# Expert weights as fp16 halves, split by ScalarE and GpSimd during the projection and the mixing

## The chip, the core and the metric

The program runs on one core of a Trainium2 chip as one launch. The metric is its time on the device in microseconds (us); the profile is of one execution of the same program.

## What is computed

One layer of a streaming encoder over 4096 prompt frames and 8 streams of 16 frames (33 tiles of 128 rows, 1024 wide). The change touches the layer's last part, a mixture of 32 experts of which each row takes two; rows are sorted by expert and cut into blocks of 128 rows that belong to one expert. From the reference:

```python
def mixer(h, ...):                       # in: rmsnorm(x); 2 head groups; out projection
    proj = h @ w_in
    xc, new_conv_l = causal_conv(x_lru, conv_l, lru_cw)
    hs, new_h = rglru(xc, h_l, ...)
    o, new_S = gdn_sequence(S_g, q, k, v, g, beta)
    return mixed @ w_out, ...

def expert_dispatch(xf, eidx, wts, w1, w3, w2):
    ...
    xb = xf[row_tok].reshape(n_blocks, ROW_BLOCK, D)
    def run(args):
        e, xblk = args
        return (jax.nn.silu(xblk @ w1[e]) * (xblk @ w3[e])) @ w2[e]
    yb = lax.map(run, (block_e, xb)).reshape(n_rows, D)
    contrib = yb[dest] * w_sorted[:, None].astype(yb.dtype)
    return jnp.zeros((T, D), yb.dtype).at[tok_sorted].add(contrib)
```

## The kernel before

The program has four phases, one after the other: projection, mixing, experts, combination. Each engine runs its own instruction list; semaphores order them. `SP` only issues DMA.

**Projection** (`project_phase`). 4096 rows go through in eight groups of 512, and the streams' 128 rows are a ninth group. Each group is cut into 24 chunks of 128 output columns, and each chunk is 24 fp16 matmuls on TensorE (three for each of eight slices of the inner dimension, because inputs and weights are held as a high and a low fp16 half: hi x hi, hi x lo, lo x hi). `sequence()` writes out by hand the order in which every engine goes through a group: Y and X chunks of the recurrent unit with their gates (`G`, `R`, `O`), Q chunks of the queries, keys and values with their convolution on VectorE and their SiLU (`S`), Z chunks of the output gate, `N` the squares of the next group's input and its norm, `B` the two decay columns. ScalarE copies a chunk from PSUM to `win` (L384), VectorE convolves it (L504 to L513). GpSimd does two small operations a group for the norm (L260, L263) and is otherwise idle. The tile `stage` (two slots of 512 KB) takes raw weights in the first group, where ScalarE and VectorE split `w_in` into halves.

**Mixing** (`mix_phase`). 33 tiles in a software pipeline; a table `MIX` says which step stands on which engine in which order in an iteration. The output projection is in halves as well. `X.Z64c` is a copy by ScalarE (`Zf`), `X.fh` and `X.fl` make the halves of the recurrent unit's output (`f_hi`, `f_lo`), `V.v` is a batched triangular inversion by VectorE, `R.x2` the residual sum (`x2b`), `R.r2` a norm on GpSimd (`rs`), `Q.sct0` a scatter of row numbers to `table` by GpSimd, `R.h2` a multiplication on GpSimd (`h2b`). The streams' state `S_s` (2 MB) is loaded at iteration 0 and used by the last tile.

**Experts** (`experts_phase`). 98 blocks. Table `EXPERTS`: TensorE does `up` of block b + 1 (8 fp32 matmuls over 512 columns, weights `w13`), the transposes `gT` of block b, the transposes `T0`, `T1` of the rows of block b + 2, then `d0`, `d1` of block b (4 fp32 matmuls, weights `w2`). ScalarE does `silu`, VectorE the product `mul`; `T0c` (ScalarE) and `T1c` (VectorE) copy transposed rows to SBUF, `gTc` (ScalarE) the transposed product, `d0c` and `d1c` the result. The weights of an expert (2 MB and 1 MB) lie in one of two slots; SP loads an expert's weights when `d1` of the last block that used the slot is through:

```python
sem_, value = at("d1", end, 1)
sp.wait_ge(sem_, value)
load_expert(sp, T, weights, pair * 2 + (2 + p), p)
...
arrived(pair * 2 + (2 + p), p)     # waits for both loads, then counts up `ready`
```

and `up` waits for `ready`.

**Combination** (`combine_phase`) gathers each row's two results and writes the output.

Of the kernel before, what the change touches and what calls it, by code (L numbers as in the profile page):

```python
# [50 lines left out]
M_SCALE = 4.0  # L51
OUT = 1.0 / (W_SCALE * M_SCALE)
W13, W2 = KD * 2 * FE, (FE // P) * D

# [45 lines left out]
def sequence():  # L100
# [6 lines left out]
    for m in range(3, QC):  # L107
        out += [("Q", m), ("S", m - 1)] + [("N", 0)] * (m == 6) + [("B", 0)] * (m == 9)
    return out + [("Z", 0), ("S", QC - 1), ("Z", 1), ("Z", 2), ("Z", 3)]


def project_phase(nc, T, gb, const, cols):
# [6 lines left out]
    with ExitStack() as ctx:  # L119
# [13 lines left out]
        junk = sb("junk", [P, D])  # L133
# [32 lines left out]

        ident = const[:, MATS.index("ident"), :]
# [33 lines left out]
        table_out = sem("table_out")  # L201

# [3 lines left out]
        def _(sp):  # L206
# [6 lines left out]
            sp.dma_start(const[:, :, :], T["mats"]).then_inc(setup_in, 16)  # L213
# [16 lines left out]
            with sp.Fori(2, groups) as g:  # L230
                load(g, GT)
            load(groups, 1)

# [3 lines left out]
            while done < n:  # L237
                w = min(n - done, GN)
                sp.dma_start(T["table"][done * P:(done + w) * P, 0].rearrange("(p n) -> p n", p=P),
                             junk[:, 0:w].bitcast(I32)).then_inc(table_out, 16)  # L240
# [10 lines left out]
        def _(pool):  # L251
# [13 lines left out]
            with pool.Fori(0, groups) as g:  # L265
                group(g, GT)
            group(groups, 1)
# [71 lines left out]
        def _(act):  # L339
# [19 lines left out]
            def group(g, nt, stream, following, first=False):  # L359
# [100 lines left out]
        def _(dve):  # L460
# [17 lines left out]
            def group(g, nt, stream, following, first=False):  # L478
# [6 lines left out]
                for kind, m in seq:  # L485
                    if first and block_of.get((kind, m), len(wblocks)) + 2 < len(wblocks):
                        split(block_of[kind, m] + 2)
                    if kind == "N" and following:
# [106 lines left out]
X.Z64.pe X.Z64c.act Y.outA3.pe R.r3.dve  # L595
# [3 lines left out]
MIX = [tuple(s.split(".")) for s in MIX]  # L599
ENGINES = ("pe", "act", "dve", "pool")  # L600


def mix_phase(nc, T, gb, const, cols, eid, rank, wts, base, start, tabs):
    NT, NB = tiles(), blocks()
    H = HEADS
    with ExitStack() as ctx:
# [5 lines left out]

        w_out_hi = sb("w_out_hi", [P, KD, D], FP16)
# [105 lines left out]

        w_out_raw = S_s[:, :, :, :].rearrange("p s h n -> p (s h n)").rearrange("p (k n) -> p k n", k=4)  # L720
# [3 lines left out]
        owner = {n: done[st, e] for st, n, e in MIX if st != "V"}  # L724
# [29 lines left out]
        route_columns = sem("route_columns")  # L754
        route_rows = sem("route_rows")
# [30 lines left out]

        def prologue(t):

            return t < LEAD
# [10 lines left out]
        def program(engine, begin, steps, inversion=None, after_first=None):  # L800
# [5 lines left out]
            def iteration(i):  # L806
                tiles_ = {st: tile_at(i, n) for st, n in (("E", LEAD + 1), ("F", LEAD), ("X", 1), ("Y", 0), ("R", -1), ("Q", -2))}
                for st, n, e in MIX:
                    if e != engine:
                        continue  # L810
                    if st == "V":
# [14 lines left out]
        def _(sp):  # L826
# [49 lines left out]
            def iteration(i):  # L876
# [6 lines left out]
                if x is not None:  # L883
                    sp.wait_ge(*at("x2", x[0], 1))
                    sp.dma_start(xr[:, :], T["x"][bass.ts(x[0], P), :]).then_inc(xr_in, 16)
                if valid and part == 0:
                    batch_load(b, n, min(i + LEAD, NT))
# [17 lines left out]

# [1201 lines left out]
```

## Time and profile before

| | us |
|---|---|
| median of three runs (least, most) | 3940.72 (3940.56, 3945.06) |
| profiled execution, its own time | 3933.96 |
| its span on the core | 3932.3 |
| TensorE busy | 3423.2 (87%) |
| VectorE busy | 1874.7 (48%) |
| ScalarE busy | 1318.6 (34%) |
| GpSimd busy | 816.6 (21%) |

In the profile PE is TensorE, DVE VectorE, ACT ScalarE, POOL GpSimd and SP SyncE; L12 is line 12 of the kernel. A tile is named without its buffer number, and `out<-in` says what an instruction writes and reads. The busy shares are averages over four phases with different limits. An fp32 matmul stands in the trace as two passes.

### The profile page before, as it was taken

To read this page: it belongs to the slowest core of one execution; us is meant where nothing else is said; L and a number is where in the kernel's file an instruction comes from. 1 tells how busy PE (TensorE), PEld (TensorE's weight loads), DVE (VectorE), ACT (ScalarE), POOL (GpSimd) and SP (SyncE) were. 2 spreads that over 40 slices of the span, in tenths; PEclk is the share of its full clock that TensorE was granted. 3 is DMA by queue.
4 is the path that set the end of the run, shared out by engine and by line. 5 is a ranking of instruction groups with operands and counts; after the bars stand their busy time and mean duration, and the time that the engine had idled before them with its cause. 6 is when DMAs were issued, how large, how long until landed. Compare 5 with 4: busy or idle time off the path is not lost. (4 is left out here: it accounts for less than half of the span.)

```text
span 3932.3 us, 57456 instructions
## 1 busy us (share of the span) xinstructions
PE 3423.2 (87%) x17482; PEld 2023.8 (51%) x17483; DVE 1874.7 (48%) x4755; ACT 1318.6 (34%) x2585; POOL 816.6 (21%) x1002
## 2 busy tenths in 40 slices
PE   7999999999995688889888899769999999999920
PEld 3444444444445677777777766534444444444410
DVE  6564465365454457777777776521111111111148
ACT  7465355355445133333333333211111111111112
POOL 0000000000000234544455444211111111111144
PEclk9999999999997599999999999979999999999965
DMA  4311111111012354444444444144555466553268
GB/s 142 119 38 52 60 45 48 56 48 51 35 54 81 101 149 120 129 139 142 131 122 135 134 121 128 44 183 181 190 217 219 170 235 229 192 200 120 88 253 326
DMA packets 335720, 513.88 MB, mean 131 GB/s; under 512 B 79968, under 2 KB 228928, under 8 KB 327104
## 3 DMA queue, kind: packets, MB, share of 16 engines
q1 hardware_dynamic: 252400, 279.19, 22.4%
q10 hardware_dynamic: 54288, 146.56, 9.4%
q0 software_dynamic: 28864, 86.09, 6.5%
q8 instruction: 81, 1.33, 0.1%
q14 instruction: 87, 0.71, 0.1%
HBM read 341.49 MB, written 170.26 MB: 130 GB/s over the span
## 5 line engine op out<-in xcount | busy, mean ns | idle before, releaser
L1761 PE MATMUL ebank<-w,rowsT 128*128 x1568 | 703.4, 602 | 33.7 <-SPq L1702 30.4
L300 PE MATMUL pP<-h_hi,w_hi 128*128 128x512 f16 (+1 forms) x1728 | 625.7, 366 | 31.4 <-DVE h_lo L482 16.8
L300 PE MATMUL pP<-h_hi,w_lo 128*128 128x512 f16 (+1 forms) x1728 | 625.1, 366 | 0.0
L300 PE MATMUL pP<-h_lo,w_hi 128*128 128x512 f16 (+1 forms) x1728 | 625.0, 366 | 0.0
L1761 PEld LDWEIGHTS ebank<-w,rowsT 128*128 128x128 f32 x1568 | 301.0, 193 | 421.9 <-issue 421.9
L1828 DVE TENSOR_TENSOR gu<-ebank,sil 128x256 f32<-128x256 f32 x98 | 41.6, 424 | 697.1 <-ACT sil L1796 697.1
L1779 PE MATMUL ebank<-w,guT 128*128 x784 | 353.4, 593 | 2.6 <-ACT guT L1800 2.6
L513 DVE SCALAR_TENSOR_TENSOR cv<-win,cols_sb,cv 128x512 f32<-128x512 f32 (+1 forms) x432 | 305.4, 707 | 35.1 <-issue 3.6
L1796 ACT ACTIVATE sil<-ebank 128x256 f32<-128x256 f32 x98 | 37.6, 384 | 819.3 <-PE ebank L1761 819.3
L300 PEld LDWEIGHTS pP<-h_hi,w_hi 128*128 128x128 f16 x1728 | 172.1, 100 | 221.1 <-issue 31.4
L300 PEld LDWEIGHTS pP<-h_lo,w_hi 128*128 128x128 f16 x1728 | 172.4, 100 | 188.0 <-issue 14.1
L300 PEld LDWEIGHTS pP<-h_hi,w_lo 128*128 128x128 f16 x1728 | 172.3, 100 | 183.4 <-issue 3.8
L260 POOL TENSOR_TENSOR ss<-ss,eps 128x4 f32<-128x4 f32 (+1 forms) x9 | 1.8, 197 | 1115.0 <-ACT junk L348 1115.0
L1779 PEld LDWEIGHTS ebank<-w,guT 128*128 128x128 f32 x784 | 140.9, 189 | 143.7 <-issue 143.7
L1833 DVE COPY yb<-ebank 128x512 f32<-128x512 f32 x98 | 67.8, 691 | 272.9 <-PE ebank L1779 272.9
L1729 POOL DMA_DIRECT2D idx<-table x98 | 55.0, 562 | 655.5 <-PE ebank L1751 651.0
L1732 POOL DMA_INDIRECT rows<-h,idx x98 | 95.5, 974 | 349.5 <-DMA idx<-table 344.4
L384 ACT ACTIVATE win<-pP 128x512 f32<-128x512 f32 (+1 forms) x144 | 80.1, 556 | 236.7 <-PE pP L300 234.1
L1309 POOL DMA_INDIRECT table<-tid,offs x66 | 69.7, 1056 | 330.4 <-DVE offs L1558 303.6
L1097 PE MATMUL bank<-w_out_hi,f_hi 128*128 128x512 f16 x264 | 100.4, 380 | 42.5 <-DVE lg L1497 42.5
L1751 PE MATMUL ebank<-const,rows 128*128 128x128 f32 x784 | 102.5, 274 | 27.0 <-DMA rows<-h,idx 27.0
L504 DVE COPY win<-carry 128x3 f32<-128x3 f32 x128 | 21.2, 165 | 219.8 <-ACT win L384 219.0
(328 smaller groups left out, 6219.8 us busy)
## 6 DMA issues: line engine op xcount, KB each, us to landing
w<-in_w SPq DMA_DIRECT2D x32, 2048.0 KB, 9.0
y<-yb ACTq DMA_DIRECT2D x98, 512.0 KB, 4.9
ft<-mixin SPq DMA_DIRECT2D x33, 1280.0 KB, 8.4
mixin<-qo ACTq DMA_DIRECT2D x128, 256.0 KB, 2.0
w<-in_w SPq DMA_DIRECT2D x32, 1024.0 KB, 12.3
xt<-in_x SPq DMA_DIRECT2D x33, 512.0 KB, 5.1
xr<-in_x SPq DMA_DIRECT2D x33, 512.0 KB, 5.1
x<-x2b ACTq DMA_DIRECT2D x33, 512.0 KB, 5.5
```

The lines of the kernel that those rows point to most:

```text
L300: ins = nc.tensor.matmul(pP[n % NPB][:, 0:N], w[:, k, c0:c0 + P], h[:, k, 0:N], start=(k + i == 0), stop=(k == KD - 1 and i == 2))
L384: nc.scalar.activation(window(c, 3, stream), shaped(pP[number[kind, m] % NPB][:, 0:N], stream), ACT.Copy, scale=PROJ).then_inc(*act_did.di ...
L513: ins = nc.vector.scalar_tensor_tensor(dst, window(c, j, stream), cw(j), dst, ALU.mult, ALU.add)
L1097: ins = nc.tensor.matmul(flat((YD, YE)[half]), f[:, c, :], w[:, c, half * 512:half * 512 + 512], start=(c + i == 0), stop=False)
L1309: pool.indirect_dma_start(T["table"], bass.IndirectOffsetOnAxis(ap=offs[k][:, 0:1], axis=0), tid[:, 0:1], None).then_inc(ids_out, 16)
L1729: pool.dma_start(idx[p][:, :], T["table"][bass.ds(where, P), :]).then_inc(idx_in[p], 16)
L1732: pool.indirect_dma_start(xb[p][:, :], None, T["h2"], bass.IndirectOffsetOnAxis(ap=idx[p][:, 0:1], axis=0)).then_inc(rows_in[p], 16)
L1751: ins = nc.tensor.transpose(bank[:, k * P:(k + 1) * P], xb[p][:, c * P:(c + 1) * P], ident)
L1761: ins = nc.tensor.matmul((M0, M1)[p][:, :], xT[p][:, k, :], w13[:, bass.ds(s, 1), k * 512:(k + 1) * 512].rearrange("p a n -> p (a n)"), st ...
L1779: ins = nc.tensor.matmul((OA, OB)[h][:, :], guT[p][:, k, :], w.rearrange("p a n -> p (a n)"), start=(k == 0), stop=(k == FE // P - 1))
L1828: nc.vector.tensor_tensor(gu[p][:, :], (M0, M1)[p][:, FE:2 * FE], sil[p][:, :], ALU.mult).then_inc(*did(n))
L1833: nc.vector.tensor_copy(yb[p][:, 512:], OB[:, :]).then_inc(*did(n))
```

## The change

Before the experts run, their weights are multiplied by 512 and split into a high and a low fp16 half, and the halves are written to a scratch array `ws` in DRAM. This is done in 192 pieces of 128 x 1024 fp32 (512 KB), six for each expert: 126 in the projection, 18 in each of seven groups, and 66 in mixing, two an iteration and three in every fifth one, in iterations 0 to 29. The experts then load halves (the same number of bytes) and do three fp16 matmuls in place of one fp32 matmul, so the rows and the product are split into halves too.

In the projection, ScalarE scales a piece in place (`W` in the sequence), GpSimd copies it to fp16 and subtracts, SP stores the two halves and loads the piece after the next one into the same slot. The norm of the next group stands on GpSimd after nine of the 18 pieces, and on VectorE at `M` (after Q10) instead of `N`. In mixing ScalarE makes the high half and the scaled piece, GpSimd the low half; `S_s` is their buffer, so the streams' state is loaded after the last piece. The constant matrices (704 KB) are loaded at the start of mixing, the projection loads only the identity (64 KB). `w13` and `w2` are loaded apart, each with its own `ready`, and the first waits only for `up` of the last block in its slot.

```diff
 def sequence():
     for m in range(3, QC):
-        out += [("Q", m), ("S", m - 1)] + [("N", 0)] * (m == 6) + [("B", 0)] * (m == 9)
+        out += [("Q", m), ("S", m - 1)] + [("N", 0)] * (m == 6) + [("M", 0)] * (m == 10) + [("B", 0)] * (m == 9)
...
+    for kind, m in out:
+        paced.append((kind, m))
+        if kind in "YXQZ":
+            c += 1
+            while n < NW and n < c * NW // 23:
+                paced.append(("W", n))
+                n += 1
...
# projection, SP
+            def experts(g):
+                for j in range(NW):
+                    q = (g - 1) * NW + j
+                    piece_store(q, j % 2)
+                    if not isinstance(q, int) or q + 2 < NC:
+                        piece_load(q + 2, j % 2)
...
# projection, GpSimd
+            def piece(g, j):
+                q, p = (g - 1) * NW + j, j % 2
+                turn = ((g - 1) * (NW // 2) + j // 2 + 1) * 16
+                pool.wait_ge(piece_scaled, q + 1)
+                pool.wait_ge(halves_out[p], turn)
+                pool.sem_inc(pieces_begun, 1)
+                raw = stage[:, p, :, :].rearrange("p k n -> p (k n)")
+                nc.gpsimd.tensor_copy(halves[:, p, 0, :], raw)
+                pool.drain()
+                nc.gpsimd.tensor_tensor(halves[:, p, 1, :], raw, halves[:, p, 0, :], ALU.subtract).then_inc(expert_split, 1)
+            def split(g, n):
+                for j in range(NW):
+                    piece(g, j)
+                    if j == AHEAD - 1:
+                        group(g + 1, n)
...
# projection, ScalarE
+                    elif kind == "W" and not first and not stream:
+                        raw = stage[:, m % 2, :, :]
+                        act.wait_ge(expert_in[m % 2], ((g - 1) * (NW // 2) + m // 2 + 1) * 16)
+                        nc.scalar.activation(raw, raw, ACT.Copy, scale=W_SCALE).then_inc(piece_scaled, 1)
...
 MIX = """
-X.Z64.pe X.Z64c.act Y.outA3.pe R.r3.dve
+X.Z64.pe X.Z64c.act Y.outA3.pe R.r3.dve W.hi.act W.lo.pool
...
# mixing, ScalarE and GpSimd
+            def high(q):
+                raw, hi = raws[q % 3], split[q % 3][:, 0:WC]
...
+                nc.scalar.activation(hi, raw, ACT.Copy, scale=W_SCALE)
+                act.drain()
+                nc.scalar.activation(raw, raw, ACT.Copy, scale=W_SCALE).then_inc(piece_hi, 1)
+            def low(q):
+                pool.wait_ge(piece_hi, q + 1)
+                nc.gpsimd.tensor_tensor(split[q % 3][:, WC:], raws[q % 3], split[q % 3][:, 0:WC], ALU.subtract
+                                        ).then_inc(piece_lo, 1)
...
 EXPERTS = """
-O.gT.pe O.gTc.act
-T.T0.pe T.T1.pe T.T0c.act T.T1c.dve
+O.gT.pe O.gTc.act O.gTl.dve
+T.T0.pe T.T1.pe T.T0c.act T.T0l.dve T.T1c.act T.T1l.dve
...
# experts, SP
-                    sem_, value = at("d1", end, 1)
-                    sp.wait_ge(sem_, value)
-                    load_expert(sp, T, weights, pair * 2 + (2 + p), p)
+                    for part, last_use in enumerate(("up", "d1")):
+                        sem_, value = at(last_use, end, 1)
+                        sp.wait_ge(sem_, value)
+                        load_part(sp, T, weights, pair * 2 + (2 + p), p, part)
...
# experts, TensorE: up (d0 and d1 likewise, and these wait for gTl and ready[1])
+        PARTS = ((0, 0), (0, 1), (1, 0))
-                        ins = nc.tensor.matmul((M0, M1)[p][:, :], xT[p][:, k, :],
...
+                        for i, (x, w) in enumerate(PARTS):
+                            ins = nc.tensor.matmul((M0, M1)[p][:, :], xT[p][:, x, k * P:(k + 1) * P],
+                                                   half(s, k // 2, w, k % 2 * 512),
+                                                   start=(k + i == 0), stop=(k == KD - 1 and i == 2))
```

On GpSimd in the projection's loop over groups, this stood in a group before (the two operations of the norm and the loop's end):

```order
L260 ISA
L260 TENSOR_TENSOR ss<-ss,eps 128x4
L262 REGISTER_ALU
L263 TENSOR_TENSOR rs<-ss,neghalf 128x4
L265 REGISTER_ALU
L265 COMPARE_AND_BRANCH
```

and this stands there now around the same norm, in the middle of the 18 pieces:

```order
L315 REGISTER_ALU
L316 ISA
L319 CAST halves<-stage 128x1024
L321 TENSOR_TENSOR halves<-stage,halves 128x1024
L305 REGISTER_ALU
L306 TENSOR_TENSOR ss<-ss,eps 128x4
L308 REGISTER_ALU
L309 TENSOR_TENSOR rs<-ss,neghalf 128x4
L315 REGISTER_ALU
L319 CAST halves<-stage 128x1024
L321 TENSOR_TENSOR halves<-stage,halves 128x1024
```

Nine copies and subtractions stand ahead of the norm, which was alone, and nine behind it.

On GpSimd at the end of an iteration of mixing (`ATf` is a masked attention tile, `table` the scatter, `T` an inverse tile from the batched inversion, `rs` the norm of the residual sum) before:

```order
L1276 TENSOR_TENSOR B<-Gin,const 128x512 x2
L1257 TENSOR_TENSOR ATf<-ATf,const 128x512
L1309 DMA table<-tid,offs 135296x1
L1268 TENSOR_TENSOR T<-Tin,const 128x128 x4
L1292 TENSOR_TENSOR rs<-s,eps 128x1
```

and now:

```order
L1392 TENSOR_TENSOR B<-Gin,const 128x512 x2
L1373 TENSOR_TENSOR ATf<-ATf,const 128x512
L1434 TENSOR_TENSOR split<-S_s,split 128x1024 x2
L1425 DMA table<-tid,offs 135296x1
L1384 TENSOR_TENSOR T<-Tin,const 128x128 x4
L1408 TENSOR_TENSOR rs<-s,eps 128x1
```

The low halves of two pieces stand between `ATf` and the scatter.

On VectorE in the experts, one block in the loop (its product, the copies of the transposed rows of a block further on, the copy of a result) before:

```order
L1827 REGISTER_ALU
L1828 TENSOR_TENSOR gu<-ebank,sil 128x256
L1822 REGISTER_ALU
L1823 ISA
L1824 COPY rowsT<-ebank 128x512
L1831 ISA
L1832 ISA
L1833 COPY yb<-ebank 128x512
```

and now:

```order
L1971 REGISTER_ALU
L1972 SCALAR_TENSOR_TENSOR gu<-ebank,sil 128x256
L1975 ISA
L1976 TENSOR_TENSOR guT<-ebank,guT 128x256
L1965 ISA
L1966 SCALAR_TENSOR_TENSOR rowsT<-ebank,rowsT 128x512
L1965 REGISTER_ALU
L1966 SCALAR_TENSOR_TENSOR rowsT<-ebank,rowsT 128x512
L1978 ISA
L1979 REGISTER_ALU
L1980 TENSOR_SCALAR yb<-ebank 128x512
```

The low half of the product (L1976) stands behind the product, and two low halves of rows stand where one copy stood.

## Rows read from the trace of the kernel before

**Rows 1.** The page's slices: TensorE's busy tenths in 40 equal parts of the span.

```profile
PE   7999999999995688889888899769999999999920
```

**Rows 2.** Timeline of GpSimd: start, us, engine, line, operation, idle before.

```profile
271.82 0.20 POOL L260 TENSOR_TENSOR ss<-ss,eps 128x4 f32<-128x4 f32 x1 [147.28 <-ACT junk L348]
...
415.11 0.20 POOL L260 TENSOR_TENSOR ss<-ss,eps 128x4 f32<-128x4 f32 x1 [141.88 <-ACT junk L348]
```

**Rows 3.** Windows, one projection group: busy us, clock, DMA share, GB/s.

```profile
272.00:415.00 143.00, 138.12 (x721) 65.02 (x719) 74.74 (x139) 70.75 (x98) 1.03 (x2) 1.00 0.14 52
```

**Rows 4.** Waits in mixing, 1300 to 2500 us: us in total, times, longest.

```profile
PE bank L1097 <- DVE lg L1497: 42.1, 23, 2.2
```

**Rows 5.** Timeline of TensorE in the experts, one block.

```profile
3562.01 7.03 PE L1761 MATMUL ebank<-w,rowsT 128*128 x16
3568.87 0.38 PE L1769 MATMUL ebank<-const,gu 128*128 128x128 f32 x2
3569.09 1.04 PE L1751 MATMUL ebank<-const,rows 128*128 128x128 f32 x8
3569.96 3.61 PE L1779 MATMUL ebank<-w,guT 128*128 x8
3573.41 7.03 PE L1761 MATMUL ebank<-w,rowsT 128*128 x16
```

**Rows 6.** Line 1796, the experts' SiLU on ScalarE, whole run: durations in ns.

```profile
L1796 ACT ACTIVATE sil<-ebank x98: 383/383/385, 2603.6 to 3751.5; 128x256 f32<-128x256 f32 x98
```

**Rows 7.** Waits in the experts, 2600 to 3750 us.

```profile
PE ebank L1761 <- SPq L1702: 30.4, 15, 2.2
```

**Rows 8.** Timeline of mixing: the fp16 matmuls of the output projection.

```profile
1712.56 0.38 PE L1110 MATMUL bank<-w_out_hi,mx_hi 128*128 128x512 f16 x1
...
1712.99 0.38 PE L1110 MATMUL bank<-w_out_hi,mx_lo 128*128 128x512 f16 x1
```

**Rows 9.** Timeline of VectorE in the same expert block.

```profile
3569.49 0.42 DVE L1828 TENSOR_TENSOR gu<-ebank,sil 128x256 f32<-128x256 f32 x1 [6.59 <-ACT sil L1796]
```

**Rows 10.** Windows, 50 us of the experts, the busiest of the DMA.

```profile
3000.00:3050.00 50.00, 50.00 (x148) 24.39 (x147) 7.75 (x13) 7.40 (x16) 7.12 (x9) 1.00 0.64 241
```

**Rows 11.** Groups of ScalarE by shape: xcount, busy us, mean ns, idle before.

```profile
L1226 ACT ACTIVATE junk<-x2b 128x1024 f16<-128x1024 f32 x33 | 34.9, 1057 | 166.7 <-DVE x2b L1481 166.7
```

**Rows 12.** Groups of GpSimd by line and shape.

```profile
L1300 POOL TENSOR_TENSOR h2b<-xn,ln_row 128x1024 f32<-128x1024 f32 x33 | 78.0, 2365 | 24.2 <-DVE xn L1487 23.1
...
L253 POOL MEMSET gates<- 128x1024 f32 x1 | 1.0, 951 | 0.4 <-POOLq L2079 0.4
```

**Rows 13.** Line 1349 on VectorE, whole run: least, median and most ns.

```profile
L1349 DVE TENSOR_TENSOR scf<-sse,rr x33: 152/3084/3107, 1262.9 to 2224.9; 128x4 f32<-128x4 f32 x33
```

**Rows 14.** Timeline of mixing around that operation, both engines.

```profile
1731.03 3.10 DVE L1349 TENSOR_TENSOR scf<-sse,rr 128x4 f32<-128x4 f32 x1
1731.73 2.36 POOL L1300 TENSOR_TENSOR h2b<-xn,ln_row 128x1024 f32<-128x1024 f32 x1
```

**Rows 15.** Timeline of VectorE in the projection: the convolution of one chunk.

```profile
420.10 2.40 DVE L513 SCALAR_TENSOR_TENSOR cv<-win,cols_sb,cv 128x512 f32<-128x512 f32 x3
```

**Rows 16.** Groups of VectorE by line and shape.

```profile
L482 DVE SCALAR_TENSOR_TENSOR h_lo<-pG,ln,h_hi 128x512 f16<-128x512 f32 x32 | 22.5, 742 | 0.1
```

**Rows 17.** DMA issues of the whole run: KB each, median us to landing.

```profile
w<-in_w SPq DMA_DIRECT2D x32, 2048.0 KB, 9.0
...
stage<-in_w_in SPq DMA_DIRECT2D x24, 512.0 KB, 4.4
...
const<-in_mats SPq DMA_DIRECT2D x1, 704.0 KB, 7.3
```

**Rows 18.** Timeline of mixing, VectorE and GpSimd at the end of an iteration.

```profile
1718.45 1.06 POOL L1309 DMA_INDIRECT table<-tid,offs  x1 [8.82 <-DVE offs L1558]
1719.01 0.68 DVE L1481 SCALAR_TENSOR_TENSOR x2b<-bank,xr 128x512 f32<-128x512 f32 x1
...
1724.52 0.18 POOL L1292 TENSOR_TENSOR rs<-s,eps 128x1 f32<-128x1 f32 x1
```

More of the change, by code:

```diff
@@ L51 @@
 M_SCALE = 4.0
+G_SCALE = 4.0
+WC = 1024
+NW = 18
+AHEAD = 9
 OUT = 1.0 / (W_SCALE * M_SCALE)
 W13, W2 = KD * 2 * FE, (FE // P) * D
+DOWN = 1.0 / (W_SCALE * G_SCALE)
+EC = (W13 + W2) // WC
 COLS = {}
@@ L785, in early_there, with pieces @@
             return (pre_in[t], 16) if t < LEAD else (qk_in[t % 2], 16 * ((t - LEAD) // 2 + 1))
+        def pieces(i):
+            return [q for q in range(LEFT) if PER[q] == i]
         def prologue(t):
@@ L810, in iteration @@
                         continue
-                    if st == "V":
+                    if st == "W":
+                        for q in pieces(i):
+                            steps[st](q)
+                    elif st == "V":
                         b, part = phase(i + LEAD)
@@ L885, in iteration @@
                     sp.dma_start(xr[:, :], T["x"][bass.ts(x[0], P), :]).then_inc(xr_in, 16)
+                for q in pieces(i - 1):
+                    piece_store(q)
+                for q in pieces(i):
+                    piece_load(q)
+                if pieces(i - 1) and not pieces(i):
+                    states()
                 if valid and part == 0:
@@ L1633, in load_expert, with load_part, experts_phase @@
 def load_expert(engine, T, weights, e, p):
-    w13, w2, loaded = weights
-    for dst, src in ((w13, "w13"), (w2, "w2")):
-        engine.dma_start(dst[:, p, :], T[src][bass.ds(e, 1)].rearrange("a p n -> p (a n)")).then_inc(loaded[p], 16)
-def experts_phase(nc, T, const, cols, eid, rank, start, dest, tabs, weights, kept):
+    ws, loaded = weights
+    for part in range(2):
+        load_part(engine, T, weights, e, p, part)
+def load_part(engine, T, weights, e, p, part):
+    ws, loaded = weights
+    c, n = ((0, W13 // WC), (W13 // WC, W2 // WC))[part]
+    engine.dma_start(ws[:, p, c:c + n, :], T["ws"][bass.ds(e * EC + c, n)].rearrange("c p n -> p c n")
+                     ).then_inc(loaded[p][part], 16)
+def experts_phase(nc, T, ident, cols, eid, rank, start, dest, tabs, weights, kept):
     NT, NB = tiles(), blocks()
@@ L1662, in experts_phase @@
         owner = {n: done[st, e] for st, n, e in EXPERTS}
-        ready = sem("expert_ready")
+        ready = [sem(f"expert_ready{c}") for c in range(2)]
         idx_in = [sem(f"idx_in{p}") for p in range(2)]
@@ L1700, in arrived @@
             def arrived(e, p):
-                sp.wait_ge(loaded[p], (e - p) * 16 + 32)
-                sp.sem_inc(ready, 1)
+                for part in range(2):
+                    sp.wait_ge(loaded[p][part], (e - p) * 8 + 16)
+                    sp.sem_inc(ready[part], 1)
             for p in range(2):
```

173 lines of the change are left out of this document (117 added, 56 removed).

## The prediction

> **What bounds the kernel now.** I read the page's slices first [rows 1]: TensorE is near full in most tenths, thinner between a third and two thirds of the span, and idle in the last slices, so each stage is to be read by what TensorE does there. The projection comes first, until about 1245 us. Its period is the distance of GpSimd's short norm chains, 143.3 us [rows 2]. In such a group TensorE is busy 138 of 143 us, VectorE 74.7, ScalarE 70.8, GpSimd 1.0 [rows 3]. TensorE bounds it, and GpSimd is free. Mixing runs from about 1250 to 2560 us; there TensorE's tenths fall to 7 or 8, and its waits are short and many, for VectorE's `lg` among others [rows 4]: a chain of steps through four engines sets its pace. The experts run from about 2600 to 3757 us. The timeline of one block shows `up` (16 passes over 512 columns, two for each fp32 matmul), transposes, `d0` and `d1` (8 passes) end to end on TensorE: 3562.01 to 3573.41, 11.40 us [rows 5]. Over the run one SiLU stands for one block: 98 of them from 2603.6 to 3751.5, (3751.5 - 2603.6)/97 = 11.83 us [rows 6]. The 0.43 us above 11.40 holds 15 waits for weights, 30.4 us in all, 0.31 a block [rows 7]. The combination at the end is not touched.
>
> **The experts: what is removed.** From the starts in [rows 5]: `up` 3568.87 - 3562.01 = 6.86, transposes of `gu` 0.22, of the rows 0.87, down 3573.41 - 3569.96 = 3.45. With fp16 halves each fp32 matmul becomes three fp16 ones: 24 for `up`, 12 for the down part. An fp16 matmul over 512 columns starts every 0.2158 us in the projection and mixing (1712.56 to 1712.99 is two of them, 0.43) [rows 8]; the granted clock is 1.00 in a projection group and in the experts [rows 3, 10]. So `up` is 24 x 0.2158 = 5.18, down 12 x 0.2158 = 2.59, and a block 5.18 + 0.22 + 0.87 + 2.59 = 8.86 us.
>
> **The experts: what is added.** `d0` now waits for the low half `gTl` on VectorE, which stands behind `guT` (now `gTc`) on ScalarE and behind the product on VectorE. The product ends at 3569.49 + 0.42 = 3569.91 [rows 9]; a 128 x 256 step of the same length behind it ends at 3570.33, and `d0` could begin at 3569.96: TensorE waits 0.37 us a block. The other new steps are two low halves of the rows on VectorE, and `T1c` moves to ScalarE. Each of the four moves 128 x 512, twice the product's 0.42 at most; they lie beside `d0`, `d1` (2.59 us) and the start of the wait before them, and cost nothing. If that cover were gone, the last of them would cost its 0.8. For weights I keep 0.15 of the 0.31 us: the loads of `up` now start when `up` of an expert's last block is through, one part of a period earlier, but periods are shorter. Sum 8.86 + 0.37 + 0.15 = 9.38, against 11.83 a gain of 2.45, times 97 = **-238 us**. Bounds: without either wait 2.97 x 97 = -288; if the experts with two blocks, of which I count one for each of the 15 waits, gain nothing, (97 - 30) x 2.45 = -164. The second is possible because an expert with two blocks moves 3 MB of weights, 2 MB of rows and results and 0.5 MB of kept rows, 5.8 MB in 18.8 us, which is 307 GB/s; the busiest 50 us now move 241 GB/s at a DMA share of 0.64 [rows 10]. By proportion that is a share of 0.82, so I take it that it fits.
>
> **The projection: what is added.** In each of seven groups 18 pieces of 512 KB go through `stage`: ScalarE scales 128 x 1024 in place (1.06 [rows 11]), GpSimd copies to fp16 and subtracts, SP stores and loads. The subtraction is a 128 x 1024 two-input operation like `h2b`: 2.37 us [rows 12]. No copy by GpSimd is in the trace. Its bounds are the nearest rows: a write of 128 x 1024 fp32 with no input, 0.95, and the two-input operation, 2.37 [rows 12]; I take 1.0, nearer the first, since one input is read and half the bytes are written. A group gets 18 x (1.0 + 2.37) = 61 us of GpSimd and 18 x 1.06 = 19 of ScalarE. ScalarE then works 70.8 + 19 = 90 of 143 us and finds room, so its part costs nothing while three PSUM banks and four windows of the convolution lie between it and TensorE; without that cover, up to 19 a group.
>
> What makes this more than work on a free engine is a lock. `scf` (two inputs in SBUF, 4 elements wide) takes 0.15 us at the least and 3.08 in the median [rows 13]; at 1731.03 it lasts 3.10 and ends with GpSimd's `h2b`, 1731.73 + 2.36 = 1734.09 [rows 14]. So a VectorE operation with two inputs in SBUF doesn't get through while GpSimd reads SBUF. The Trainium skill, SBUF — State Buffer, section Who interferes with whom, states this as an exclusive lock for the whole instruction, whoever issues first; the trace agrees (3084 against 152 ns). By that rule alone, were no idle time of VectorE found, the pieces would add 7 x 61 = 427 us; by the rows, with the idle time, it is the term below. In the projection the convolution's multiply-adds are such operations (2.40 us for three [rows 15]), as are most gate steps; of the 74.7 us a group, eight low halves of the input at its start read PSUM (8 x 0.74 = 5.9 us [rows 16]), which leaves 69 us to be shared. 61 + 69 = 130 us has to lie between the first convolution and the end of the last chunk, some 124 us (143 less the transposes and the first chunks, some 19). It doesn't fit by 6 us, and two streams that hold each other up don't pack without gaps: by hand, with pieces after the chunks that the order gives, I get 13 us a group, 7 x 13 = **+91 us**. Bounds: 0 if the pieces pack into VectorE's idle time (61 + 74.7 = 136 < 143); with a copy of 2.37, 18 x 4.74 + 69 = 154 against 124, 30 a group, +210.
>
> The Trainium skill, GPSIMD Engine Reference, section Engine selection, says that GpSimd is about half as fast as VectorE with two inputs and about line rate with one. By that the copy would be near 0.9 us (an estimate of mine from that page) and the projection would lose some 11 us a group; no run here shows the copy.
>
> The norm of the next group moves behind nine pieces on GpSimd and four chunks later on VectorE. Its cover is the rest of the group, over 30 us; a piece is under 5, so it costs nothing unless pieces fall two chunks behind. The pieces' DMA is 18 x 1.05 MB = 19 MB a group, 132 GB/s beside 52 now [rows 3], below the 241 of the experts, so it is hidden. A slot's round (scale 1.06, GpSimd 3.4, store and load at about 4.4 each [rows 17]) is near 13 us, and two slots give a piece every 6.7, which is the pace wanted: little slack, and part of the 13 us.
>
> **Mixing: what is added.** Two pieces, in every fifth iteration three, in 30 iterations. ScalarE's two operations a piece (2.1 us) stand between `Zf` and `f_hi`; TensorE still has the last output matmuls of the old iteration to do behind `Zf`, some 4 us of them, so I put this at nothing; without that cover it is 4.2 an iteration. GpSimd is idle before `table` at 1718.45 (its idle time there is 8.82 us) [rows 18], so 2 x 2.37 = 4.7 us fit; but VectorE has its inversion and `f_lo` in the same microseconds, small operations with two inputs in SBUF. They are held until about 1719 and then end some 4.7 us late, so the second half of `x2b`, which ends at 1719.69 [rows 18], ends at about 1724.4. ScalarE's squares of it take 1.06 [rows 11], and with half a microsecond for their accumulator and the handing on GpSimd could begin its `rs` at 1721.3, where it begins at 1724.52 [rows 18]: 3.2 us of slack, so 4.7 - 3.2 = 1.5 us lost. 30 x 1.5 = **+45 us**; bounds 0 (GpSimd slips between) and +110 (3.7 an iteration: no slack, and three pieces).
>
> **At nothing.** `mats` loads at the start of mixing instead of at the start of the projection: landing 7.3 us [rows 17], beside the first tile's loads of about the same; at the start the first transposes wait for `x` anyway. Without cover, 7 us. `S_s` (2 MB) is loaded after the last piece, for the last tile, more than an iteration ahead; the 9.0 us that 2 MB of weights take [rows 17] lie in it. Without cover, 9 us.
>
> **Sum.** -238 + 91 + 45 = -102. Against the profiled execution's 3933.96 us (span 3932.3) that is 3832; the median shown is 6.8 higher, 3940.72, and the forecast on it is **3839 us**. 0.2% is 8 us, about what can be told from no change.
>
> **The rivals.**
> - *The lock costs little.* VectorE is idle half of every group [rows 3], and TensorE has three banks of lead. Then 5 us a group and 0.3 an iteration: 3940.7 - 238 + 35 + 10 = 3748. Against it: 130 us in 124. Chance 0.26.
> - *Experts bound by transfers.* Experts with two blocks gain nothing: 3940.7 - 164 + 136 = 3913. For it speaks the 307 GB/s wanted; against it a share of only 0.64 now. The wait of `up` for `ready` would grow well above 30 us. Chance 0.10.
> - *Slower: GpSimd's copy is dear.* If it costs as much as the subtraction, GpSimd and VectorE together bound the projection: 3940.7 - 238 + 210 + 45 = 3958. It decides once the projection loses (238 - 45)/7 = 27.6 a group, that is a copy of 1.0 + (27.6 - 13)/18 = 1.8 us. Chance 0.16, most of it beyond 0.2%.
> - *My forecast*, 3839, has the remaining 0.48; its own range is 3790 to 3890.
>
> **Range and chances.** 3725 to 3965 takes in the three rivals and the bounds of the projection; left out are the cases in which two bounds come together, as experts without waits with a lock that costs nothing, or a dear copy with mixing at its +110, 2 in 10 in all. The dear copy gives slower 0.14 and a part of same, 0.06; faster is the rest, 0.80.
>
> **What would show it.** Starts of the norm chains about 156 us apart (143 if the lock is hidden, 165 and more if the copy is dear); the copy's row near 1.0; `scf`-like stretched rows at the convolution; TensorE's idle time before `d0` of about 0.37 for VectorE; SiLUs 9.4 us apart; iterations of mixing 1.5 us longer, with `x2b` the late one. I am wrong if the copy is over 1.8 us, or if TensorE's fp16 passes in the experts don't start every 0.216 us.

## The result, and the profile after

The median of four runs is 3911.11 us (3905.95 to 3916.06), that of the kernel before beside them 3940.64; the ratio is 0.993, with a 95% interval of 0.991 to 0.995. So the change made the kernel faster, by 29.5 us, where 102 were forecast. The span of the profiled execution is 3910.6 us, 21.7 less than before.

Where they come from can be read from three marks that both traces have: `lg` of the router on VectorE (33 times, once for each tile of mixing), the SiLU of the experts (98 times), and the end. Until the first `lg` the kernel after needs 1563.2 us in place of 1451.0 (+112.2, the projection above all); from the first to the last `lg` 1154.9 in place of 1099.0 (+55.9, mixing); from there to the first SiLU 4.6 less; from the first to the last SiLU 966.0 in place of 1147.9 [rows 6] (-181.9, the experts); behind it 3.3 less. All three terms of the forecast have the right sign, and all three were too good: +91, +45 and -238 were forecast.

The experts' SiLU after (line, count, least/median/most ns, first and last start), which answers to [rows 6]:

```profile
L1938 ACT ACTIVATE sil<-ebank x98: 384/385/385, 2767.1 to 3733.1; 128x256 f32<-128x256 f32 x98
```

(3733.1 - 2767.1)/97 = 9.96 us a block, where 9.38 were forecast. TensorE's timeline of one block, beside [rows 5]:

```profile
3568.59 5.35 PE L1897 MATMUL ebank<-ws_sb,rowsT 128*128 x24 [0.68 <-issue]
3573.78 0.38 PE L1905 MATMUL ebank<-ident,gu 128*128 128x128 f32 x2
3574.00 1.04 PE L1887 MATMUL ebank<-ident,rows 128*128 128x128 f32 x8
3575.32 2.76 PE L1918 MATMUL ebank<-ws_sb,guT 128*128 x12 [0.28 <-DVE guT L1976]
3578.36 3.84 PE L1897 MATMUL ebank<-ws_sb,rowsT 128*128 x17 [0.28 <-issue]
```

`up` takes 3573.78 - 3568.59 = 5.19 us (5.18 forecast). `d0` waits for the low half of the product: the trace shows 0.28 us of idle time, and in the terms of the forecast, from start to start, it is 3575.32 - 3574.00 - 0.87 = 0.45 (0.37 forecast). What nobody costed stands in the first and the last row: ahead of `up` TensorE is idle for 0.28 us, in every second block 0.68, and waits for nothing but its own sequencer ("issue"). The sequencer's rows in that gap (PEldq; the two lines that load the expert's number and its slot into registers):

```profile
L1890 PEldq TENSOR_LOAD <-tab_expert x1: 307/307/307, 3576.5 to 3576.5; - x1
L1890 PEldq SEQ_ASSERT  x1: 18/18/18, 3577.1 to 3577.1; - x1
...
L1891 PEldq TENSOR_LOAD <-tab_slot x1: 301/301/301, 3577.3 to 3577.3; - x1
L1891 PEldq FUSED_REGOPS  x1: 151/151/151, 3577.7 to 3577.7; - x1
L1891 PEldq SEQ_ASSERT  x1: 18/18/18, 3577.9 to 3577.9; - x1
```

The two loads and the waits of `up` fill the time from 3576.4 to 3578.3, 1.9 us; the matmuls of `d0` and `d1`, all issued by then, start one behind the other until 3575.32 + 12 x 0.2158 = 3577.91. From there to the next `up` are 0.45 us here, and 0.85 where 0.68 is shown. In the kernel before the same loads ran at 3570.5 and 3571.2, under down matmuls that lasted until 3573.41 [rows 5].

The projection's period after, by GpSimd's norm (beside [rows 2]), and the windows of one group (beside [rows 3]):

```profile
754.36 0.20 POOL L306 TENSOR_TENSOR ss<-ss,eps 128x4 f32<-128x4 f32 x1 [16.78 <-ACT junk L414]
...
914.94 0.20 POOL L306 TENSOR_TENSOR ss<-ss,eps 128x4 f32<-128x4 f32 x1 [16.79 <-ACT junk L414]
```

```profile
627.00:788.00 161.00, 143.20 (x722) 66.63 (x721) 108.23 (x140) 88.88 (x116) 64.37 (x38) 0.96 0.46 163
```

The two rows are 160.6 us apart, and three groups (from 432.69) take 160.7 each, in place of 143.3. VectorE is busy 108.2 us in place of 74.7, though it has no operation more: its convolution is held up. TensorE's 722 matmuls take 143.2 us, where 721 took 138.1 [rows 3]: some 5 us more of work, at a granted clock of 0.96 in place of 1.00. The timeline of one convolution, VectorE and GpSimd:

```profile
666.54 4.73 DVE L583 SCALAR_TENSOR_TENSOR cv<-win,cols_sb,cv 128x512 f32<-128x512 f32 x3
666.68 1.50 POOL L319 CAST halves<-stage 128x1024 f16<-128x1024 f32 x1 [17.17 <-ACT stage L443]
668.33 2.39 POOL L321 TENSOR_TENSOR halves<-stage,halves 128x1024 f16<-128x1024 f32 x1
```

Three operations take 4.73 us beside one piece, where they took 2.40 [rows 15]. That is the lock that the prediction read from [rows 13, 14]. It isn't kept to operations with two inputs: a copy of three columns with one input is held too (one of them from 766.80 to 768.37, beside a subtraction by GpSimd that ends at 768.34), here after and before (least/median/most ns):

```profile
L574 DVE COPY win<-carry x128: 155/169/2090, 34.1 to 1264.9; 128x3 f32<-128x3 f32 x128
...
L504 DVE COPY win<-carry x128: 158/168/171, 37.2 to 1154.2; 128x3 f32<-128x3 f32 x128
```

The first of the two GpSimd rows above is the copy by GpSimd that no trace had shown; over the run:

```profile
L319 POOL CAST halves<-stage x126: 1031/1212/1600, 185.4 to 1280.1; 128x1024 f16<-128x1024 f32 x126
L321 POOL TENSOR_TENSOR halves<-stage,halves x126: 2120/2383/2399, 187.1 to 1281.3; 128x1024 f16<-128x1024 f32 x126
```

The second new thing is the 16.78 us for which GpSimd stands at the norm. The order of GpSimd has the norm behind nine pieces, ScalarE's order has the squares for it behind eleven scalings. Both slots are full by then, and the price is paid on ScalarE:

```profile
754.19 0.58 ACT L454 ACTIVATE win<-pP 128x512 f32<-128x512 f32 x1
763.79 1.06 ACT L443 ACTIVATE stage<-stage 128x1024 f32<-128x1024 f32 x1 [9.03 <-DMA stage<-in_we]
```

ScalarE waits 9.03 us in its order for a piece that can be loaded only when GpSimd is through with the one before it in the same slot, and behind it stand the copies that free TensorE's banks. Some 20 us later TensorE is idle for such a copy, and when it starts again its granted clock is near the lower of its two levels, 1.2 GHz (windows of 6 us; the columns as in [rows 3]):

```profile
779.80 1.28 ACT L493 ACT_TABLE_LOAD   x1 [4.82 <-DVE asum L620]
...
785.05 0.61 PE L366 MATMUL pP<-h_hi,w_hi 128*128 128x512 f16 x1 [7.78 <-ACT win L454]
...
777.00:783.00 6.00, 0.27 (x2) 0.00 (x0) 2.60 (x3) 3.08 (x6) 1.22 (x1) 0.92 0.72 259
783.00:789.00 6.00, 3.95 (x10) 1.45 (x11) 3.92 (x9) 5.25 (x7) 0.00 (x0) 0.51 0.12 44
```

The wait of ScalarE is only a part of this idle time: just ahead of the copy ScalarE waits 4.82 us more, for a step (`asum`) that VectorE has behind its stretched convolutions.

In mixing, the end of one iteration on the three engines, beside [rows 18]:

```profile
2014.77 2.15 DVE L1513 TENSOR_TENSOR vp<-va,vt_ 128x48 f32<-128x48 f32 x1
2017.00 2.02 DVE L1516 TENSOR_TENSOR vt_<-vt_,vp 128x48 f32<-128x48 f32 x1
...
2014.73 4.22 POOL L1434 TENSOR_TENSOR split<-S_s,split 128x1024 f16<-128x1024 f32 x2 [4.65 <-ACT S_s L1351]
...
2022.36 3.79 PE L1161 MATMUL bank<-S,ft 128*128 128x128 f32 x16 [3.63 <-DVE offs L1680]
```

While GpSimd subtracts twice, VectorE gets through two operations of the inversion that take 0.21 us elsewhere; all behind them, `offs`, `f_lo` and `x2b`, is late, and TensorE waits 3.63 us. The Trainium skill, SBUF — State Buffer, section Who interferes with whom, states it so (two inputs in SBUF against a GpSimd operation that reads SBUF); these rows agree, 2.15 against 0.21 us. The held inversion was forecast, the step that TensorE then waits for was not: it is `offs` (73.5 us in 29 places of mixing, 1.1 in 5 before), not the chain of `x2b`, squares and norm. Nor was what follows. The 16 matmuls of the last row take 3.79 us; an iteration earlier they took 2.05. After the idle time the granted clock is 0.51 for a while, and over the whole of mixing (first row before, second after, from the first to the last `lg`) TensorE's work is 26.3 us longer for the same matmuls:

```profile
1451.00:2550.00 1099.00, 978.49 (x6976) 769.75 (x6976) 800.67 (x2679) 397.90 (x1099) 503.74 (x633) 0.99 0.43 124
...
1563.00:2718.00 1155.00, 1004.82 (x6977) 796.38 (x6976) 866.14 (x2680) 520.28 (x1227) 640.84 (x697) 0.96 0.56 177
...
2022.00:2028.00 6.00, 5.64 (x26) 5.64 (x27) 4.43 (x17) 2.78 (x7) 4.62 (x8) 0.51 0.56 138
```

### The profile page after: what moved, and what is told of

Its sections match the earlier page's. It is cut to its first block and busy times, and to the rows that moved or that the text cites. A ratio compares the mean times of both kernels' runs of the same rounds, so it can differ in the third digit from the quotient of the medians.

```text
span 3910.6 us, 64191 instructions
## 1 busy us (share of the span) xinstructions
PE 3248.1 (83%) x18658; PEld 1969.3 (50%) x18659; DVE 2266.1 (58%) x4951; ACT 1615.6 (41%) x2941; POOL 1403.2 (36%) x1320
## 5 line engine op out<-in xcount | busy, mean ns | idle before, releaser
L1897 PE MATMUL ebank<-ws_sb,rowsT 128*128 x2352 | 527.1, 381 | 50.7 <-issue 45.5
L583 DVE SCALAR_TENSOR_TENSOR cv<-win,cols_sb,cv 128x512 f32<-128x512 f32 (+1 forms) x432 | 441.0, 1021 | 35.0 <-issue 3.6
L1897 PEld LDWEIGHTS ebank<-ws_sb,rowsT 128*128 128x128 f16 x2352 | 230.4, 98 | 347.1 <-issue 101.6
L319 POOL CAST halves<-stage 128x1024 f16<-128x1024 f32 x126 | 155.2, 1231 | 578.1 <-ACT stage L443 578.1
L1918 PE MATMUL ebank<-ws_sb,guT 128*128 x1176 | 270.6, 380 | 31.0 <-DVE guT L1976 31.0
L321 POOL TENSOR_TENSOR halves<-stage,halves 128x1024 f16<-128x1024 f32 x126 | 287.1, 2279 | 18.9 <-issue 1.7
L1918 PEld LDWEIGHTS ebank<-ws_sb,guT 128*128 128x128 f16 x1176 | 114.6, 97 | 161.9 <-issue 53.8
L443 ACT ACTIVATE stage<-stage 128x1024 f32<-128x1024 f32 x126 | 132.4, 1051 | 103.8 <-DMA stage<-in_we 92.1
L1161 PE MATMUL bank<-S,ft 128*128 128x128 f32 x512 | 84.2, 332 | 73.5 <-DVE offs L1680 73.5
L1966 DVE SCALAR_TENSOR_TENSOR rowsT<-ebank,rowsT 128x512 f16<-128x512 f32 x196 | 126.4, 686 | 21.3 <-ACT rowsT L1933 10.5
```

The costliest lines, as they stand in the source:

```text
L319: nc.gpsimd.tensor_copy(halves[:, p, 0, :], raw)
L321: nc.gpsimd.tensor_tensor(halves[:, p, 1, :], raw, halves[:, p, 0, :], ALU.subtract).then_inc(expert_split, 1)
L443: nc.scalar.activation(raw, raw, ACT.Copy, scale=W_SCALE).then_inc(piece_scaled, 1)
L583: ins = nc.vector.scalar_tensor_tensor(dst, window(c, j, stream), cw(j), dst, ALU.mult, ALU.add)
L1161: ins = nc.tensor.matmul(bank[:, h, :], ft[p][:, (H if n == "KS" else 0) + h, :], S[:, h, :], start=True, stop=True)
L1897: ins = nc.tensor.matmul((M0, M1)[p][:, :], xT[p][:, x, k * P:(k + 1) * P], half(s, k // 2, w, k % 2 * 512), start=(k + i == 0), stop=(k = ...
```

## The experiments

All times are medians beside runs of the kernel before on the same chip (3935 to 3940); "after" is the changed kernel, 3911.

**The wait ahead of `up`: a rotated loop.** TensorE's order in the experts becomes, for block b:

```diff
-up(b+1); gT(b); T0, T1(b+2); d0, d1(b)                 # register loads ahead of up and of d0
+gT(b); T0, T1(b+2); loads for up(b+2) and d0(b); d0, d1(b); up(b+2)
```

> Experts alone: TensorE's loop is rotated, so that `up` of a block stands at the end of the part before it and its two register loads stand beside those of `d0`, where TensorE waits for `gTl` anyway; the loop's branch then lies behind `up`. Theory (TensorE's sequencer can't hide 1.9 us of register loads and branch behind 12 fp16 matmuls): the idle time before `up` (0.28 and 0.68 us) goes, a block falls from 9.96 to about 9.3 us, and the time by some 60 us to 3850. Rival (the extra time a block is waiting for weights or DMA): no change, 3911 within 8.

Measured: 3888.83, ratio 0.986 (0.984 to 0.989). The idle time ahead of `up` is gone, but there is a new one. TensorE's timeline:

```profile
3570.90 1.04 PE L1887 MATMUL ebank<-ident,rows 128*128 128x128 f32 x8
3572.81 2.76 PE L1920 MATMUL ebank<-ws_sb,guT 128*128 x12 [0.88 <-DVE guT L2008]
```

A block takes 9.66 us, half of the way to the 9.3 expected. That `gTl` alone makes the wait of 0.88 is unlikely, since nothing on VectorE has changed; four register loads now stand ahead of `d0`. The next run tests it.

**One load in place of two.** The same with the slot taken from the expert's number:

```diff
-up_regs[1] = pe.value_load(tabs["slot"][0:1, bass.ds(b, 1)], min_val=0, max_val=1)
+up_regs[1] = pe.snap(up_regs[0] % 2)
...
-pe_slot[0] = pe.value_load(tabs["slot"][0:1, bass.ds(b, 1)], min_val=0, max_val=1)
+pe_slot[0] = pe.snap(e % 2)
```

> The rotated loop of the run before, with one register load where there were two: the slot is worked out from the expert's number in the sequencer. Theory (TensorE's sequencer is what `d0` waits for in the rotated loop, 0.88 us, since four register loads stand ahead of it): the wait falls to the 0.3 us of `gTl`, a block from 9.66 to about 9.1 us, the time from 3889 to about 3830. Rival (`gTl` itself is late): the wait stays, 3889 within 8.

Measured: 3861.70, ratio 0.981 (0.979 to 0.982); SiLUs from 2772.8 to 3682.8, 9.38 us a block. TensorE's timeline:

```profile
3570.35 1.04 PE L1887 MATMUL ebank<-ident,rows 128*128 128x128 f32 x8
3571.72 2.76 PE L1920 MATMUL ebank<-ws_sb,guT 128*128 x12 [0.33 <-DVE guT L2008]
3574.32 5.34 PE L1899 MATMUL ebank<-ws_sb,rowsT 128*128 x24
3579.50 0.38 PE L1907 MATMUL ebank<-ident,gu 128*128 128x128 f32 x2
```

So a new place for the register loads and half their number take 0.58 us off a block, as much as the forecast was wrong by: TensorE's sequencer is shown as the cause. The block doesn't reach the 9.1 us expected here, since `d0` still starts 3571.72 - 3570.35 - 0.87 = 0.50 us late.

**The loads of the weights together again.**

```diff
-for part, last_use in enumerate(("up", "d1")):
+for part, last_use in enumerate(("d1", "d1")):
```

> Undoes one part of the change: the load of `up`'s weights waits for `d1` of the slot's last block again, as that of the down weights does. Theory (loading apart hides the transfers behind the shorter blocks): an expert with two blocks has 10 us for 2 MB that take 9, so `up` waits for `ready` in some 15 experts, 15 to 30 us in all, time 3926 to 3941. Rival (the transfers fit anyway): no change, 3911 within 8.

Measured: 3932.26, ratio 0.998 (0.997 to 0.999): 21 us lost. TensorE's wait for SP's `ready`, beside [rows 7]:

```profile
PE ebank L1897 <- SPq L1839: 23.3, 15, 2.2
```

With the loads apart this wait is 0.7 us in the whole run. Of the change's gain of 29 us, 21 hang on this part, as expected.

**The norm behind eleven pieces.**

```diff
-AHEAD = 9
+AHEAD = 11
```

> Projection alone: GpSimd does the next group's norm after 11 pieces instead of 9, that is behind all pieces that ScalarE scales before the squares. Theory of the hold (GpSimd stands 16.8 us at the norm, the two slots fill, and ScalarE then waits in its order for a piece's load, 12.9 us a group): those waits fall below 3 us a group, a group takes 148 to 150 us instead of 160.7, and the time falls by some 75 us to about 3835. Theory of the lock (VectorE's convolution is held up by GpSimd, 17.4 us a group): GpSimd's work is the same, a group stays at 160 and the time at 3911 within 10.

Measured: 3890.07, ratio 0.987 (0.984 to 0.989). ScalarE's waits for loads fall as expected, from 12.9 to 2.7 us a group (51.5 and 10.8 in four), but the group only from 160.7 to 157.0 (the norm on VectorE):

```profile
618.82 5.39 DVE L538 TENSOR_SCALAR xt<-xt,rs 128x1024 f32<-128x1024 f32 x4
...
775.80 5.39 DVE L538 TENSOR_SCALAR xt<-xt,rs 128x1024 f32<-128x1024 f32 x4
```

Neither theory's number came (148 to 150 and 160). The hold is real and costs 3.7 us a group; most of the time isn't there, since what ScalarE no longer waits for, VectorE's convolution holds up next: ScalarE's waits for `cv` rise from 55.5 to 83.5 us in the same four groups.

**GpSimd's work left out in the projection.**

```diff
-nc.gpsimd.tensor_copy(halves[:, p, 0, :], raw)
-pool.drain()
-nc.gpsimd.tensor_tensor(halves[:, p, 1, :], raw, halves[:, p, 0, :], ALU.subtract).then_inc(expert_split, 1)
+pool.sem_inc(expert_split, 1)
...
+nc.gpsimd.memset(halves[:, :, :, :], 0.0)
```

> GpSimd's copy and subtraction are left out in the projection (126 pieces of halves are zeros); ScalarE's scaling, the norm's place and all transfers stay. Theory of the lock: a group goes back to 143 to 145 us and the time to about 3796. Theory of the hold: the slots still fill at the norm, and a group keeps 5 to 8 us of its 17.4: 149 to 152 us, time about 3840 to 3855.

Measured: 3809.92, ratio 0.967 (0.964 to 0.970); the three groups between the norms at 438.40 and 875.43 take 145.7 us each, and no multiply-add of the convolution is above 0.754 us. So 15 of the 17.4 us a group go with GpSimd's work, and ScalarE's scaling and 132 GB/s of transfers cost 2.4 at most. With the run before: 3.7 the hold, 11.3 the lock with the norm in its better place, 2.4 the rest. The parts hang together: ScalarE still waits 6.7 us for loads in a group here (414 to 560 us), and without the lock all that is left costs 2.4. With the lock goes the low clock, too: 722 matmuls of that group take 140.1 us at a granted clock of 0.99, 727 with the norm behind eleven pieces (592 to 749 us) 144.0 at 0.95.

**Copy or subtraction?** The high half by ScalarE, GpSimd only subtracts; norm behind eleven.

```diff
# ScalarE
+act.wait_ge(halves_out[m % 2], ((g - 1) * (NW // 2) + m // 2 + 1) * 16)
+nc.scalar.activation(halves[:, m % 2, 0, :], raw.rearrange("p k n -> p (k n)"), ACT.Copy,
+                     scale=W_SCALE)
+act.drain()
 nc.scalar.activation(raw, raw, ACT.Copy, scale=W_SCALE).then_inc(piece_scaled, 1)
...
# GpSimd
-nc.gpsimd.tensor_copy(halves[:, p, 0, :], raw)
-pool.drain()
```

> Projection alone, norm after 11 pieces as in the run with that: ScalarE writes the high half in an operation of its own (two of 1.05 us a piece, as in mixing), GpSimd only subtracts (2.3 us a piece where copy and subtraction held 3.5). Theory (what is left of the loss, 13.7 us a group, goes with the time that GpSimd reads): 13.7 x 2.3/3.5 = 9, a group takes about 152 us, time 3855. Rival (the subtraction alone, which has two inputs, holds VectorE): no change against 157.0 us and 3890. ScalarE's 19 us more a group could also take back some of it.

Measured: 3884.22, ratio 0.986 (0.984 to 0.989), a group 157: no change, the rival's number. But ScalarE was busy 107 us of a group, so the run can't tell the rival from ScalarE's cost. The next one takes that away (the factor also goes from the pieces of mixing and from the scales of SiLU and product):

```diff
-DOWN = 1.0 / (W_SCALE * G_SCALE)
+DOWN = 1.0 / G_SCALE
...
-nc.scalar.activation(raw, raw, ACT.Copy, scale=W_SCALE).then_inc(piece_scaled, 1)
+act.wait_ge(halves_out[m % 2], ((g - 1) * (NW // 2) + m // 2 + 1) * 16)
+nc.scalar.activation(halves[:, m % 2, 0, :], raw.rearrange("p k n -> p (k n)"), ACT.Copy,
+                     ).then_inc(piece_scaled, 1)
...
```

> Projection, as the run in which ScalarE writes the high half and GpSimd only subtracts, but without the factor of 512 on the expert weights (taken out of the experts' scales too), so that ScalarE has one operation of 1.05 us a piece again instead of two. Theory (there the 19 us more of ScalarE a group took back what GpSimd's shorter reading gave): a group falls from 157 to about 152 us, time about 3850. Rival (the subtraction with its two inputs does the holding, the copy little): a group stays at 156 to 157 us, time 3880 to 3890.

Measured: 3848.86, ratio 0.978 (0.976 to 0.980), and a group of 153.6 us:

```profile
605.14 4.61 DVE L538 TENSOR_SCALAR xt<-xt,rs 128x1024 f32<-128x1024 f32 x4
...
758.75 4.61 DVE L538 TENSOR_SCALAR xt<-xt,rs 128x1024 f32<-128x1024 f32 x4
```

The loss above 143.3 falls from 13.7 to 10.3 us when GpSimd works 2.3 us on a piece instead of 3.5. So the copy has a part in the loss, and the loss falls with the time for which GpSimd reads (0.75 of it is left, where the theory had 0.66); that it falls in proportion, one pair of runs doesn't show.

**The low half by VectorE in the projection.**

```diff
# ScalarE: the high half, scaled; GpSimd: the norm alone; VectorE, behind the chunk's convolution:
+elif kind == "W" and not first and not stream:
+    dve.wait_ge(piece_scaled, (g - 1) * NW + m + 1)
+    nc.vector.scalar_tensor_tensor(halves[:, m % 2, 1, :], stage[:, m % 2, :, :].rearrange("p k n -> p (k n)"),
+                                   W_SCALE, halves[:, m % 2, 0, :], ALU.mult, ALU.subtract
+                                   ).then_inc(expert_split, 1)
```

> Projection alone: GpSimd does nothing for the pieces; ScalarE writes the high half (scaled) and VectorE makes the low half in one operation (as it does for the input weights, 1.22 us each, 22 us a group). Everything is computed. Theory of the lock: the holding was dearer than the work, VectorE's 75 + 22 = 97 us fit in a group, which takes 146 to 150 us; time 3811 to 3836. Rival (VectorE's work is on the path one for one): 143.3 + 22 = 165 us a group, time about 3940.

Measured: 3836.32, ratio 0.975 (0.973 to 0.978). Three groups between the norms at 443.09 and 892.55 take 149.8 us each. VectorE's 22 us of work cost 6.5 a group, where GpSimd's 63 us on an engine that was free cost 17.4, or 13.7 with the norm behind eleven pieces; the 2.4 of scaling and transfers are in all three.

**Mixing: the low half left out, and by VectorE.**

```diff
-nc.gpsimd.tensor_tensor(split[q % 3][:, WC:], raws[q % 3], split[q % 3][:, 0:WC], ALU.subtract).then_inc(piece_lo, 1)
+w = WC if q < 3 else 2
+nc.gpsimd.memset(split[q % 3][:, WC:WC + w], 0.0).then_inc(piece_lo, 1)
```

> GpSimd's subtraction is left out in mixing (a write of two columns in its place, so the low halves of 66 pieces are not computed); ScalarE's four operations and the transfers stay. Theory of the lock: the inversion's stretched operations (2.1 us each) go back to 0.2 us, an iteration from 36.1 to about 34.5 us, time 3911 - 50 = 3861. Rival (ScalarE's operations ahead of `f_hi` or the transfers): the iteration stays at 36, time 3905 to 3911.

Measured: 3869.08, ratio 0.982 (0.979 to 0.985). `lg` in this kernel (33 of them, so 32 iterations):

```profile
L1619 DVE TENSOR_TENSOR lg<-bank,cols_sb x33: 178/180/192, 1560.5 to 2674.9; 128x32 f32<-128x32 f32 x33
```

(2674.9 - 1560.5)/32 = 34.83 us an iteration, against 36.09 after and 34.34 before: 1.26 of the 1.75 us are GpSimd's subtraction, 0.5 ScalarE's operations or the transfers, which no run here tells apart. With the subtraction go the low clock and the long matmuls: TensorE is busy 982.5 us between these marks at 0.99 (978.5 before, 1004.8 after).

```diff
-X.Z64.pe X.Z64c.act Y.outA3.pe R.r3.dve W.hi.act W.lo.pool
+X.Z64.pe X.Z64c.act Y.outA3.pe R.r3.dve W.hi.act
...
-Y.outB2.pe ... X.fh.act X.fl.dve
+Y.outB2.pe ... X.fh.act X.fl.dve W.lo.dve
```

> Mixing alone: ScalarE writes the high half only, VectorE makes the low half behind `f_lo` in one operation (1.22 us, two or three an iteration), GpSimd does nothing for the pieces. Theory of the lock: the inversion is free again, the 2.4 us lie in the 3.2 us of slack behind `x2b`, an iteration takes 34.4 to 35.0 us instead of 36.1, time 3860 to 3876. Rival (VectorE's work is on the path one for one): 34.3 + 2.4 to 2.7 = 36.8 us, time about 3935.

Measured: 3898.02, ratio 0.990 (0.988 to 0.992):

```profile
L1612 DVE TENSOR_TENSOR lg<-bank,cols_sb x33: 178/180/181, 1565.2 to 2700.1; 128x32 f32<-128x32 f32 x33
```

35.47 us an iteration. Between the two theories (34.4 to 35.0 and 36.8): no operation of the inversion's first line takes more than 1.11 us (2.16 after), but `x2b` and `xb` stand behind 2.35 us more of VectorE's own work, and TensorE's wait for `xb` (29.7 us in 20 places) takes the place of that for `offs` (73.5 in 29). Of the 36 us that mixing is still longer than before, TensorE's matmuls take 33: 1011.7 us at a granted clock of 0.96, where they took 978.5 at 0.99.

**The three mendings together**, rotated loop with one load, low halves on VectorE in both phases:

> The three mendings together: rotated loop with one register load a step in the experts, low halves on VectorE in projection and mixing; everything is computed. If the causes are separate, the parts add: 3911 - 49 - 75 - 13 = 3774, within 10. If they share one (a transfer that is late for all, say), less: above 3790.

Measured: 3760.13, ratio 0.956 (0.954 to 0.958): 151 us below the changed kernel, where the parts sum to 137, and below the 3764 to 3784 expected. The marks of the traces (`lg`, SiLU) say that the parts do add: against the kernel after, the experts are 56.0 us shorter here and in the run with one load, mixing 20.1 here and 20.0 with its low half on VectorE, the projection 77.2 here and 73.5 with its own. The single runs' times showed less of it because stages that they don't touch came out longer, as mixing by 6.2 us in the run with one load. So the three don't share a cause.

## Why the prediction was right and wrong

- *The experts, -238 forecast, -182 measured.* The step that failed is the sum 8.86 + 0.37 + 0.15 = 9.38, where 9.96 was measured: it took 36 fp16 matmuls for end to end because each starts 0.216 us behind the one before, which they do, and put nothing for what the sequencer does ahead of `up`. That was 0.45 and 0.85 us in turn, 0.65 a block. The register loads were there before and hidden, and the text named no work that hides them. It was the longer fp32 matmuls, and the change took them away. The other terms were near: the wait of `d0` 0.45 for 0.37, that for weights 0.7 us in the whole run for 0.15 a block. With the loads mended a block takes 9.38, the forecast number, and that is partly luck: the wait of `d0` is then 0.50, and none for weights is left, where the sum had 0.37 and 0.15.
- *The rival that the experts are bound by transfers* is out, though the 3911 measured is close to the 3913 that it gave: TensorE waits 0.7 us for weights in all, in stretches with a DMA share of up to 0.85. That holds because of the loads apart.
- *The projection, +91 forecast, +112 measured (17.4 us a group for 13).* The lock was right in mechanism. With the norm behind eleven pieces a group loses 13.7 us, near the 13, but not by the forecast's terms alone: 11.3 go with GpSimd's work and 2.4 with scaling and transfers, which the sum put at nothing, and in the 13.7 are some 5 us of longer matmuls at a granted clock of 0.95, for which it had no term. The copy came out at 1.03 to 1.60 us, median 1.21, for the 1.0 taken. What failed is "costs nothing unless pieces fall two chunks behind": the norm's new place makes them fall behind in every group, because ScalarE's order has two pieces more ahead of the squares than GpSimd's has ahead of the norm. That is 3.7 us a group, 26 in all.
- *The rival that the lock costs little* is out by the left-out halving (145.7 against 160.7 us a group); *the dear copy* by its own rows.
- *Mixing, +45 forecast, +56 measured.* The held inversion was right, and GpSimd's subtraction is 1.26 of the 1.75 us an iteration (1.5 forecast). The path was not: the forecast let `x2b`, its squares and the norm decide, with 3.2 us of slack, and TensorE waits for `offs`, which stands behind the same inversion. Nor was the sum, which counts the six iterations with three pieces like the others; by its own numbers they lose 7.1 - 3.2 = 3.9 us each, and the term is 24 x 1.5 + 6 x 3.9 = 59. And 26 of the 56 us are longer matmuls at a lower granted clock, for which it had no term. That the size came out near is partly luck.
- The total was wrong by more than any single term, since three errors of 56, 21 and 11 us had one sign. The larger two hold effects put at nothing: the sequencer, the hold at the norm, and the clock. The clock's part is some 7 x 5 + 26 = 61 us of longer matmuls in the projection and mixing (an estimate from the windows above; not all of it need lie on the path, and no run here has the waits without the low clock). The time lies in the stated range, 3725 to 3965, but not in the forecast's own, 3790 to 3890.

## What to carry to other kernels

When an engine's work gets shorter, list what was hidden under the long version on its own sequencer, register loads and branches too, and check that the short version still covers it. An idle GpSimd isn't free room beside a busy VectorE that works in SBUF: 22 us of work on VectorE cost less than 63 on GpSimd. Where TensorE waits some microseconds in every turn, read the granted clock behind the wait and cost the slower matmuls too. When two engines go through one order with different places for a common step, count how many items each has ahead of it: here the difference was two, as many as there were slots, so ScalarE had none to go on with and waited 12.9 us a group; with the same count on both sides 2.7 were left.

## What the runs showed of the hardware that I had not expected

- A value read from a table in SBUF into TensorE's registers takes about 0.7 us of its sequencer (0.30 the load, 0.15 the operations behind it, and smaller ones), in series with the issue of matmuls; with four of them ahead of `d0` the idle time there was 0.88 us, with two 0.33, and the trace puts both down to VectorE.
- GpSimd's own operations vary as well: its subtraction takes 2.12 us at the least and 2.38 in the median, its copy 1.03 and 1.21. What makes the difference was not looked into.
- After an idle time of 7.78 us in the projection TensorE's granted clock was 0.51 from 783 to 789 us, and after one of 3.63 us in mixing 0.51 from 2022 to 2028, where 16 matmuls took 3.79 us for 2.05. Such an idle time can cost more than its own length; it needn't, since an iteration earlier the same 16 took 2.05 after an idle time of 3.01.
